# Four extra weight tiles ahead of each expert stage, and the ring of weight tiles seated four slots further on

## The reference, cut to what matters

```python
def ec_moe(h, w_router, w_gate, w_up, w_down):   # h: 1 x 256 x 1024, 16 experts
    cap = EC_CAPACITY_FACTOR * n // N_EXPERTS     # 32 tokens for each expert
    aff = softmax(h @ w_router, axis=-1)
    g, idx = top_k(aff.swapaxes(1, 2), cap)
    xs = h[idx]                                   # 32 rows for each expert
    a = silu(xs @ w_gate) * (xs @ w_up)           # 1024 x 1024 each, float32
    y = (a @ w_down) * g                          # 1024 x 1024
    return scatter_add(y, idx)
```

## Time and profile before

| | us |
|---|---|
| median of 3 runs | 1860.04 (1857.64 to 1860.96) |
| the profiled execution's own time | 1857.91 |
| its span | 1854.4 |
| TensorE busy in the span | 1513.9 (82%) |
| VectorE busy | 536.0 (29%) |
| ScalarE busy | 319.9 (17%) |

### The profile page before, as it was taken

The page is one execution under the profiler, slowest core; times in us unless marked ns, Lnnn a source line. Parts: engine busy times, 40 slices in busy tenths (PEclk is TensorE's granted clock), DMA queues, the critical chain, the costliest instruction groups (busy, mean ns, idle before and its releaser), DMA issues. The chain is left out here.

```text
span 1854.4 us, 27443 instructions
## 1 busy us (share of the span) xinstructions
PE 1513.9 (82%) x11332; PEld 1032.6 (56%) x11332; DVE 536.0 (29%) x1085; ACT 319.9 (17%) x564; POOL 26.6 (1%) x52
## 2 busy tenths in 40 slices
PE   5999877877877878788787777777878979879998
PEld 2787456443433434388644344343437747668997
DVE  1135464101101101057411011011112256445554
ACT  2000432000000000053300000000012232244443
POOL 4000100000000000000000000000000000000000
PEclk8999998888888878799888888888789987979999
DMA  9975682899999999984499999999995420335550
GB/s 327 371 283 181 253 310 91 349 421 421 422 422 422 422 422 422 408 258 162 157 374 422 422 422 422 421 422 422 422 407 171 131 80 12 108 97 180 185 180 23
DMA packets 146826, 549.34 MB, mean 296 GB/s; under 512 B 10654, under 2 KB 79248, under 8 KB 97488
## 3 DMA queue, kind: packets, MB, share of 16 engines
q1 hardware_dynamic: 143376, 542.18, 74.7%
q10 hardware_dynamic: 1824, 4.83, 0.7%
q0 software_dynamic: 1568, 1.51, 0.5%
HBM read 547.44 MB, written 1.05 MB: 296 GB/s over the span
## 5 line engine op out<-in xcount | busy, mean ns | idle before, releaser
L654 PE MATMUL bank<-ring,scratch 128*32 128x256 f32 x4096 | 290.0, 453 | 34.1 <-DVE scratch L1224 34.1
L678 PE MATMUL bank<-ring,scratch 128*32 128x512 f32 x1024 | 175.2, 846 | 113.9 <-DMA ring<-in_moe_w_down 110.9
L654 PEld LDWEIGHTS bank<-ring,scratch 128*32 128x32 f32 x4096 | 148.7, 130 | 163.7 <-issue 102.7
L476 PE MATMUL bank<-ring,hT 128*128 128x256 f32 (+1 forms) x832 | 188.0, 387 | 4.5 <-DMA ring<-in_attn_w_in 3.5
L476 PEld LDWEIGHTS bank<-ring,hT 128*128 128x128 f32 x832 | 160.8, 196 | 29.9 <-issue 4.3
L678 PEld LDWEIGHTS bank<-ring,scratch 128*32 128x32 f32 x1024 | 45.7, 148 | 219.5 <-issue 219.5
L582 PE MATMUL bank<-scratch_split,ring_split 128*128 128x256 f32 x1344 | 160.2, 280 | 7.3 <-DVE ring_split L1271 2.9
L582 PEld LDWEIGHTS bank<-scratch_split,ring_split 128*128 128x128 f32 x1344 | 158.7, 191 | 10.1 <-issue 4.8
L1726 ACT ACTIVATE scratch<-bank 128x256 f32<-128x256 f32 x32 | 12.3, 383 | 853.4 <-PE bank L654 853.4
L688 PE MATMUL bank<-scratch 128*128 128x512 f32 x256 | 117.5, 601 | 31.1 <-DVE scratch L1246 31.1
L643 PEld LDWEIGHTS bank<-scratch,xn 128*128 128x128 f32 x1024 | 132.0, 205 | 16.5 <-issue 16.5
(11 more groups left out here) (359 smaller groups left out, 1206.5 us busy)
## 6 DMA issues: line engine op xcount, KB each, us to landing
ring<-in_moe_w_gate SPq DMA_DIRECT2D x128, 1024.0 KB, 16.1
ring<-in_moe_w_up SPq DMA_DIRECT2D x128, 1024.0 KB, 22.2
ring<-in_moe_w_down SPq DMA_DIRECT2D x128, 1024.0 KB, 18.9
ring<-in_ada_w SPq DMA_DIRECT2D x48, 1024.0 KB, 10.9
ring<-in_w_ff SPq DMA_DIRECT2D x32, 1024.0 KB, 5.2
ring<-in_conv_w_in SPq DMA_DIRECT2D x12, 1024.0 KB, 11.9
ring<-in_attn_w_in SPq DMA_DIRECT2D x10, 1024.0 KB, 14.3
ring<-in_w_in SPq DMA_DIRECT2D x7, 1024.0 KB, 11.9
```

The lines of the kernel that those rows point to most:

```text
L476: mm = nc.tensor.matmul(T[:, t * 256:t * 256 + width], lhs[:, k, t * P:(t + 1) * P], W[:, k, :], start=(k == ks[0]), stop=(k == ks[-1]))
L654: mm = nc.tensor.matmul(GU[32 * j:32 * j + 32, m * 256:(m + 1) * 256], xs[:, k, :], ring[:, s, (k % 2) * D + j * 256:(k % 2) * D + (j + 1) ...
L678: mm = nc.tensor.matmul(Y[n][32 * j:32 * j + 32, :], actT[:, b, 32 * j:32 * j + 32], ring[:, down[j][0], b * D + n * 512:b * D + (n + 1) * ...
```

## The change

Four more places for a weight unit are named: `S` at 42, at 8 and at 0 KiB, and the whole of `hT`. Each gets a semaphore (`extra_landed`). The units (1, 0) to (1, 3) of each layer go there, once in the layer. SP issues them right behind expert 0's twelve units. It waits before each for the last reader of that space: in layer 0 the products `ao11`, `ao11`, `o0T.2` and `lgp0`, in layer 1 `conv_b.3`, `out1.3`, `out1.3` and `lgp1`.

Every later unit is seated four ring slots further on. (1, 4) takes the slot of (0, 0), (1, 5) that of (0, 1), up to (1, 11) in that of (0, 7). (2, 0) to (2, 3) take the slots of (0, 8) to (0, 11), and (2, 4) that of (1, 4). From (2, 4) on every load again waits for the unit twelve places before it. `base` becomes a list with one entry for each stage, because the seats move by 8 slots (`TAIL`) in each layer.

TensorE's experts 0 and 1 are written out and the loop runs over 2 to 15. SP writes out the loads of experts 0, 1 and 2 and loops over 3 to 15. `lg_parts` moves from 43 to 41 KiB and the residual's `tmp` from 42 to 40 KiB, out of the first extra unit's way.

```diff
-        lg_parts = carve(S, 43, SEQ)
+        lg_parts = carve(S, 41, SEQ)
+        extra = [carve(S, 42, UNIT), carve(S, 8, UNIT), carve(S, 0, UNIT), carve(HT, 0, UNIT)]
...
-        base = seat["moe0"] % SLOTS
+        base = [(seat["moe0"] + TAIL * l) % SLOTS for l in range(3)]
...
-        def expert_slot(l, s):
-            return seats[seat[f"moe{l}"] + s][:2]
+        def expert_unit(l, e, s):
+            if isinstance(e, int) and e == 1 and s < 4:
+                return extra[s], extra_landed[s], 16 * (l + 1)
+            i = s if isinstance(e, int) and e == 0 else (s + TAIL) % SLOTS
+            q, filled = seats[seat[f"moe{l}"] + i][:2]
+            return ring[:, q, :], landed[q], e * 16 + 16 * (filled - (1 if i >= TAIL and not isinstance(e, int) else 0))
...
-            with pe.Fori(0, NEXP) as e:
+            def expert(e):
...
+            expert(0)
+            expert(1)
+            with pe.Fori(2, NEXP) as e:
+                expert(e)
...
-                tmp = carve(S, 42, TT, 256)
+                tmp = carve(S, 40, TT, 256)
...
                         load_expert(0, s)
-                    with sp.Fori(1, NEXP) as e:
+                    left = (("ao11", "ao11", "o0T.2", "lgp0"), ("conv_b.3", "out1.3", "out1.3", "lgp1"))[l]
+                    for s in range(4):
+                        product(sp, left[s])
+                        load_expert(1, s)
+                    for s in range(4, SLOTS):
+                        sp.wait_ge(MOE_READ, 12 * e0 + s - 3)
+                        load_expert(1, s)
+                    for s in range(SLOTS):
+                        sp.wait_ge(MOE_READ, 12 * e0 + (9 + s if s < 4 else 13 + s))
+                        load_expert(2, s)
+                    with sp.Fori(3, NEXP) as e:
                         for s in range(SLOTS):
                             sp.wait_ge(MOE_READ, e * 12 + (12 * (e0 - 1) + s + 1))
                             load_expert(e, s)
```

More of the change, by code:

```diff
@@ L324, in build @@
         landed = [sem(f"landed{s}") for s in range(SLOTS)]
+        extra_landed = [sem(f"extra_landed{i}") for i in range(len(extra))]
         unit_read = sem("unit_read")
@@ L397, in build @@
         for l, (n, shift) in enumerate(((len(CONV_ORDER), 0), (n_unit - seat["moe1"] - SLOTS * NEXP, SLOTS - TAIL))):
+            g = seat[f"moe{l}"]
             for i in range(SLOTS):
-                g = seat[f"moe{l}"] + i
-                take_seat(g, (base + i) % SLOTS, NEXP, g + SLOTS * (NEXP - 1))
-            g = seat[f"moe{l}"] + SLOTS * NEXP
+                times, s = (NEXP, i + 4) if i < TAIL else (NEXP - 1, i - TAIL)
+                take_seat(g + i, (base[l] + i) % SLOTS, times, g + SLOTS * (NEXP - 1) + s)
+            g += SLOTS * NEXP
             for i in range(n):
-                take_seat(g + i, (base + shift + i % TAIL) % SLOTS)
+                take_seat(g + i, (base[l + 1] + shift + i % TAIL) % SLOTS)
         def seating(g):
             return seats[g]
-        spare = [ring[:, (base + i) % SLOTS, :] for i in range(SLOTS - TAIL)]
+        spare = [ring[:, (base[2] + i) % SLOTS, :] for i in range(SLOTS - TAIL)]
         mem_raw, mem_n, memT = carve(spare[0], 0, TT, D), carve(spare[1], 0, TT, D), carve(spare[2], 0, KD, SEQ)
@@ L412, in build @@
         decay, pmT = carve(spare[0], 0, 4, 2, SEQ), carve(spare[1], 0, 4, 2, SEQ)
-        w_parts = [[[ring_split[:, (base + at + i) % SLOTS, :] for i in (a, a + 1)] for a in (0, 2)]
-                   for at in (TAIL, 0)]
+        w_parts = [[[ring_split[:, (base[1 + p] + at + i) % SLOTS, :] for i in (a, a + 1)] for a in (0, 2)]
+                   for p, at in enumerate((TAIL, 0))]
         unit_parts_read = ({}, {})
         release = {}
-        def expert_slot(l, s):
-            return seats[seat[f"moe{l}"] + s][:2]
+        def expert_unit(l, e, s):
[4 more added lines that the diff above has]
+            return ring[:, q, :], landed[q], e * 16 + 16 * (filled - (1 if i >= TAIL and not isinstance(e, int) else 0))
         def slot(pe, key, *shape):
@@ L650, in pe_moe @@
                         if k % 2 == 0:
-                            s, filled = expert_slot(l, 4 * m + k // 2)
-                            pe.wait_ge(landed[s], e * 16 + 16 * filled)
+                            W, there_sem, count = expert_unit(l, e, 4 * m + k // 2)
+                            pe.wait_ge(there_sem, count)
                         for j in range(4):
@@ L655, in pe_moe @@
                                 GU[32 * j:32 * j + 32, m * 256:(m + 1) * 256], xs[:, k, :],
-                                ring[:, s, (k % 2) * D + j * 256:(k % 2) * D + (j + 1) * 256],
+                                W[:, (k % 2) * D + j * 256:(k % 2) * D + (j + 1) * 256],
                                 start=(k == 0), stop=(k == KD - 1))
@@ L670, in pe_moe @@
                 pe.wait_ge(actT_ready, e + (e0 + 1))
-                down = [expert_slot(l, 8 + j) for j in range(4)]
-                for s, filled in down:
-                    pe.wait_ge(landed[s], e * 16 + 16 * filled)
+                down = [expert_unit(l, e, 8 + j) for j in range(4)]
+                for _, there_sem, count in down:
+                    pe.wait_ge(there_sem, count)
                 for n in range(2):
@@ L679, in pe_moe @@
                                 Y[n][32 * j:32 * j + 32, :], actT[:, b, 32 * j:32 * j + 32],
-                                ring[:, down[j][0], b * D + n * 512:b * D + (n + 1) * 512],
+                                down[j][0][:, b * D + n * 512:b * D + (n + 1) * 512],
                                 start=(b == 0), stop=(b == 1))
@@ L2030, in load_expert @@
                             mats[s // 4][e][(s % 4) * 256:(s % 4 + 1) * 256, :]
-                        q = expert_slot(l, s)[0]
-                        sp.dma_start(ring[:, q, :], rows.rearrange("(p a) n -> p (a n)", a=2)).then_inc(landed[q], 16)
+                        dst, there_sem, _ = expert_unit(l, e, s)
+                        sp.dma_start(dst, rows.rearrange("(p a) n -> p (a n)", a=2)).then_inc(there_sem, 16)
                     for s in range(SLOTS):
```

## The result

| | before | after |
|---|---|---|
| median of 4 runs each, us | 1859.28 | 1837.46 (1835.66 to 1837.88) |
| profiled execution's own time, us | 1857.91 | 1837.48 |
| its span, us | 1854.4 | 1835.3 |
| TensorE waits for down units in L678 (L687 after) | 110.9 us, 28 times | 99.8 us, 26 times |

The ratio is 0.9877, with a 95% interval from 0.9864 to 0.9890: 1.2% or about 22 us faster. The forecast was 1840.1 us with a range of 1836.5 to 1845.0. The direction was right and the time lies in the range, 1 us above its lower end, but the gain is some 2 us larger than the sum gave. Where these 2 us come from is one question of the experiments. The others are whether the gain is the shift into the idle stretch and not the ring's depth, and where it would end.

A forecast was written before the change was run, and what follows sets the result against it. The DMA's weight loads at 421 to 422 GB/s were taken to bound the two expert stages. 2 x (-9.94) + 0 = -19.9 us, so 1860.0 - 19.9 = 1840.1 us, range 1836.5 to 1845 us.

The forecast's parts named there:

- The term of the sum: Expert stages: four units loaded in the DMA's idle stretch ahead, 2.486 us each, make each layer 9.94 us shorter.
- full shift: Both expert stages: the whole 9.94 us is gained in each layer, time 1840.1 us; the forecast itself, 88%.
- the slacks: Experts 1 to 3: time to spare before a load leaves the DMA idle, 1.4 to 3.0 us.
- No gap in the DMA: Experts 1 to 3: slots come free in time; slack in layer 0 1.8 us at (2, 4), 2.4 at (3, 0).
- What is late next: TensorE's waits for down units: none at expert 2, about 1.4 us at expert 3; 26 waits, 95 us in all.
- The code written out: Extra loop bodies to fetch: below 0.1 MB, 0.2 us for a layer, taken as nothing.
- the sum passed the shift on unchanged: Behind each expert stage: the shift goes through the convolution stage and second block at full size, nothing added.
- The range: Full shift's own 1837 to 1843 us: stage ends -2.5 to +0.9, code and targets +1.4, runs -2.4 and +0.9.
- Packets in the loop: Expert loop: its code is fetched once and stays; instruction packets inside the loop would prove the forecast wrong.
- The rival of a refetch in each turn: Expert loops: written-out code makes each turn fetch again; at 7.5 us a turn +34 us, 1894 us; 2%.
- Too-late slots: Experts 0 to 2: TensorE runs slower, slots come free too late, gain cut; half of it gives 1850 us; 8%.
- No other engine took the gain: Stage end: rival that another engine, not the last unit, ends the stage; no change, 1860 us; 2%.

The follow-up runs named there:

- late loads: Changed kernel, but the four extra units' loads wait until expert 0's first unit has been read; 1862.09 us, ratio 1.0018; repeated 1859.16 us, ratio 1.0004.

## Where the prediction was right and where not, point by point

**The term of the sum.** Lengths of the stages, all kernels with a profile:

| units loaded ahead | layer 0 | layer 1 | shorter by | predicted |
|---|---|---|---|---|
| none (6 and 7 profiles) | 453.6 | 454.0 | | |
| 2 | 448.7 | 449.1 | 4.9 and 4.9 | 5.0 |
| 4 (4 and 3 profiles) | 443.9 | 444.0 | 9.7 and 10.0 | 9.94 |
| 8 (4 of them not loaded) | 443.3 | 442.2 | 10.3 and 11.8 | 11.1 |

The first three rows are the full shift: 2.4 to 2.5 us for each unit moved. The first row is a mean over different kernels. In layer 1 they run from 453.4 us (before, and with late loads) to 454.8 us (TensorE's code written out, nothing extra), so four units are worth 9.3 to 10.8 us there, by the partner that is taken. The last row is the limit that the slacks foretold. The late loads (453.2 to 453.5 us with four extra seats) show that it is the moment of loading that counts. The whole-kernel times follow with 1845.7 us for two and 1848.7 us for one layer. Spans are a weaker witness. Four units bring 1854.4 us (20 runs with written-out code and none, standard error 0.7) to 1835.0 us (13 runs, 0.6): 19.4 us, where 19.9 were forecast. Against the kernels with late loads (1858.9 us) the same four units make 23.9 us, so the closeness of 19.4 is partly the choice of the partner. The Trainium skill ("DMA: Bandwidth & Descriptors", section "Where 436 GB/s comes from") would by its rate have made it 23.4 us, an estimate. The steady parts of the stages ran at 421 to 422 GB/s with none, two, four and eight units, so the row decides.

**No gap in the DMA.** Right; the slacks in layer 0 were a little larger than worked out. (2, 4) landed 7.9 us after its issue and (3, 0) 8.2 us after, so each had some 3 us over the 4.9 us of an empty queue, where I had 1.8 and 2.4.

**What is late next.** Right in kind: no wait at expert 2, a first one at expert 3. It was 2.73 us and not 1.4. Of this, 0.46 us stand there without a wait too; TensorE's own cadence was 24.04 and 24.11 us, not 24.26, which makes 0.5 us over three experts; and the units landed 0.4 us later, counted from the first gate matmul. The wait ahead of L687 came 26 times as forecast, 99.8 us in all and not 95.

**The code written out: the term that was mis-sized.** This is the step of the sum that failed. I took nothing for it, at most 0.2 us of loss for a layer, and I kept the 3.5 us outside the span as they were. The time outside the span fell. It was 2.95 us in the mean of 68 runs of the kernel before (2.1 to 4.5) and 2.17 us in 20 runs with TensorE's code written out and no extra units (2.1 to 2.2 in each). That makes 0.8 us, and 1.3 us in the two profiled executions. It goes with the layout of TensorE's code: that code alone brings it, SP's alone doesn't. An instruction packet behind the last recorded instruction is in both profiles with the old TensorE code and in none of the twelve with the new one. That the time is spent on this packet is likely, but not shown.

**The rest of the span: open.** The mean span was 1856.5 us before (standard error 0.3) and 1835.0 us after, 21.5 us less. The stages account for 18.8 us (profiled pair) to 19.7 us (means of the table), so some 2 to 3 us more were gained elsewhere in the span, where the sum passed the shift on unchanged. Which part of the change does it is not shown. The written-out code is one candidate, with 1854.4 us in 20 runs, 2.1 us below the kernel before (standard error 0.8). But the 20 runs with late loads have the same written-out code, and their stages are as long as before, and their mean span is 1858.9 us. So kernels that should be equal differ in their means by 4.4 us, twice what is to be explained. The profiles show where such differences lie. The same instructions from layer 1's last down matmuls to the end took 466.3 us with TensorE's code alone, 472.7 us in the kernel before and 472.0 to 475.9 us in three executions of the changed one. The two profiled executions before and after differ by 20.4 us: 9.5 and 9.3 in the stages, 1.3 outside the span and 0.3 in all the rest together.

**The range.** Its upper end follows from its terms (1840.1 + 0.9 + 1.4 + 0.9 = 1843.3). The lower end doesn't: the terms named give 1840.1 - 2.5 - 2.4 = 1835.2, and I wrote 1837. That the measured 1837.46 us lies in the range stated, 1836.5 to 1845.0, in spite of a term taken at nothing is in part luck.

**Packets in the loop.** As forecast, the instruction queue is nearly silent in the stage: 2 packets from 375 to 780 us (at 382 and 388 us, ahead of expert 2's down matmuls), then none. The rival of a refetch in each turn is out.

**The other rivals.** Too-late slots cost nothing at four units and most of the rest at eight. No other engine took the gain.

## What to carry to other kernels

Where a stage is bound by its transfers, look at the transfer engine's idle time directly ahead of it: each unit that could be loaded there was worth its transfer time here (2.4 to 2.5 us of 2.49), and dead scratch space that is free for only that moment served for it. Before adding more, walk through the issue times of the first loads: a unit is worth nothing from the point on where the slot of a later load comes free too late (here behind the fourth to fifth). When a small edit also writes code out, measure that alone; here 0.8 us outside the span went with the layout of TensorE's code. And take more than one partner: two kernels without the gain differed by 4.4 us in their mean spans, while the lengths of their stages agreed within 1.5 us.

## What the runs showed of the hardware

- The end of a kernel can come with an instruction fetch. In the two profiled executions with a packet of the instruction queue 2.2 to 2.5 us behind the span's end, the time outside the span was 3.5 and 3.7 us; in the twelve without it, it was 2.1 to 2.2 us. Over all runs it was 2.1 to 5.4 us with the old TensorE code and 2.1 to 2.2 us with the new one. The Trainium skill ("Runtime: NRT & Kernel Launch", section "Instruction fetch mechanics") calls the crossing of a 16 KiB boundary mostly hidden. In the body the traces agree: over the two packets at 382 and 388 us TensorE's cadence was 24.11 us, and 24.04 us for the expert before. For the very end no run shows whether the added time is spent on the fetch.
- Idle stretches of 2.3 to 7.0 us ahead of the down matmuls left them 1.3 to 3.0 us longer than the 3.64 us at the granted clock of 1.00 (2.4 GHz), in all profiles here; three matmuls into a free bank, which cut the idle stretch to 0.3 to 0.7 us, removed that.
- A convolution stage of the same instructions took 146.4 us at a mean granted clock of 0.90 (kernel before) and 151.4 us at 0.85 (first profile with late loads); the profile with eight units has 150.6 us at 0.85. Differences of 5 us in a span of 1855 can come from that alone, which is why lengths of a stage, not spans, had to decide here.
